# The products of a matmul unit alternate between two PSUM banks instead of filling one bank after the other

## The reference

```python
ada = (c @ w_ada + b_ada)[:, None, :]
sh1, sc1, g1, sh2, sc2, g2 = jnp.split(ada, N_ADA, axis=-1)
u = x * (1 + sc1) + sh1
proj = u @ w_in                                  # 2048 x 8192
z_p, x_c, b_c, c_c, gate_p, gate_c = jnp.split(proj, [o1, o2, o3, o4, o5], axis=-1)
y_p, new_pool = _pool_mixer(z_p, pool_hist, pos, pool_grp_w, pool_scale)
y_p = y_p @ w_pool_up                            # 1024 x 2048
y_c, new_conv = _short_conv(c_c * x_c, conv_hist, conv_w)
y_c = (b_c * y_c) @ w_conv_up                    # 1024 x 2048
mixed = (jax.nn.sigmoid(gate_p) * y_p + jax.nn.sigmoid(gate_c) * y_c) @ w_o
x = _layernorm(ALPHA * x + g1 * mixed, ln1_g, ln1_b)
u2 = x * (1 + sc2) + sh2
h = jnp.square(jax.nn.relu(u2 @ w_ff1 + b_ff1))  # 2048 x 8192
x = _layernorm(ALPHA * x + g2 * (h @ w_ff2 + b_ff2), ln2_g, ln2_b)
```

## Time and profile before

| | |
|---|---|
| median of three runs | 1459.07 us |
| the profiled execution | 1459.57 us, of which its span is 1457.7 |
| mean granted clock of TensorE | 0.997 |
| PE busy | 1442.0 us (99%), 11815 matmuls |
| PEld busy | 1362.0 us (93%) |
| DVE busy | 853.1 us (59%) |
| ACT busy | 531.0 us (36%) |
| POOL busy | 100.6 us (7%) |

### The profile page before, as it was taken

How to read it: one execution, slowest core, us unless ns; L and a number is a source line. 1 busy time by engine, 2 the same in 40 slices (tenths; PEclk the granted TensorE clock), 3 DMA queues, 4 the chain that set the end, 5 groups by cost and what they waited for, 6 DMA issues and landing times.

```text
span 1457.7 us, 27550 instructions
## 1 busy us (share of the span) xinstructions
PE 1442.0 (99%) x11815; PEld 1362.0 (93%) x11815; DVE 853.1 (59%) x1037; ACT 531.0 (36%) x385; POOL 100.6 (7%) x99
## 2 busy tenths in 40 slices
PE   8999999999999999999999999999999999999998
PEld 6899989888888898997899999999999999999997
DVE  4677665565678656449755545454545544454557
ACT  3333223233325223235634333443334433343435
POOL 1000000000440000000050000000000000000800
PEclk9999999999999999999999999999999999999999
DMA  9987888887886786886755555555566555655541
GB/s 316 385 287 275 301 316 311 304 319 274 326 323 245 276 330 245 338 305 233 258 174 179 188 180 173 180 188 180 173 180 187 180 173 181 188 178 173 183 163 61
DMA packets 149727, 343.61 MB, mean 236 GB/s; under 512 B 6037, under 2 KB 16313, under 8 KB 141434
## 3 DMA queue, kind: packets, MB, share of 16 engines
q1 hardware_dynamic: 147986, 340.36, 67.8%
q0 software_dynamic: 752, 1.31, 0.3%
q10 hardware_dynamic: 912, 0.85, 0.2%
HBM read 340.19 MB, written 2.79 MB: 235 GB/s over the span
## 4 chain that ended last, share of the span: by engine, by line
PE 96%; DVE 2%; SPq 1%; DMA 0%; ACT 0%; issue 0%; DVEq 0%; ACTq 0%
PE main L1601 30%; PE main L1602 30%; PE main L1603 30%; PE ps_ada L1635 2%; PE ps_ada L1717 1%; PE ps_adat L1717 1%; PE ps_a L1717 1%; SPq L431 1%; DMA Uf<-in_x_prompt 0%; DVE w_lo L1017 0%; DVE G L1460 0%; ACT w_hi L700 0%; DVE U L1492 0%; DVE G L1454 0%; PE ps_a L1796 0%
## 5 line engine op out<-in xcount | busy, mean ns | idle before, releaser
L1017 DVE TENSOR_TENSOR w_lo<-raw,w_hi 128x2048 fp32r<-128x2048 f32 (+1 forms) x212 | 483.4, 2280 | 458.3 <-ACT w_hi L700 457.8
L700 ACT ACTIVATE w_hi<-raw 128x2048 fp32r<-128x2048 f32 (+1 forms) x227 | 429.8, 1894 | 870.4 <-PE main L1603 856.9
L1601 PE MATMUL main<-U,w_hi 128*128 128x264 f32 x2320 | 662.7, 286 | 3.0 <-issue 1.3
L1603 PE MATMUL main<-U,w_lo 128*128 128x264 f32 x2320 | 660.0, 284 | 0.0
L1602 PE MATMUL main<-U,w_hi 128*128 128x264 f32 x2192 | 621.3, 283 | 0.0
L1601 PEld LDWEIGHTS main<-U,w_hi 128*128 128x128 f32 x2320 | 436.9, 188 | 31.1 <-issue 27.3
L1603 PEld LDWEIGHTS main<-U,w_lo 128*128 128x128 f32 x2320 | 436.4, 188 | 0.0
L1602 PEld LDWEIGHTS main<-U,w_hi 128*128 128x128 f32 x2192 | 413.0, 188 | 0.0
L1601 PE MATMUL main<-H,w_hi 128*128 128x264 f32 x1280 | 365.1, 285 | 0.0
L1603 PE MATMUL main<-H,w_lo 128*128 128x264 f32 x1280 | 362.5, 283 | 0.0
L1602 PE MATMUL main<-H,w_hi 128*128 128x264 f32 x1152 | 327.5, 284 | 0.0
(11 more groups left out here) (271 smaller groups left out, 629.2 us busy)
## 6 DMA issues: line engine op xcount, KB each, us to landing
raw<-in_w_ff SPq DMA_DIRECT2D x128, 1024.0 KB, 5.2
ada_raw<-in_w_ada SPq DMA_DIRECT2D x64, 1024.0 KB, 6.7
raw<-in_w_in SPq DMA_DIRECT2D x63, 1024.0 KB, 9.4
Uf<-in_w_ada SPq DMA_DIRECT2D x18, 1024.0 KB, 9.6
raw<-in_w_o SPq DMA_DIRECT2D x16, 1024.0 KB, 8.9
raw<-in_w_pool_up SPq DMA_DIRECT2D x8, 1024.0 KB, 9.6
raw<-in_w_conv_up SPq DMA_DIRECT2D x8, 1024.0 KB, 9.8
PB<-in_w_ada SPq DMA_DIRECT2D x6, 1024.0 KB, 11.2
```

Of the source, the lines that this page charges most:

```text
L700: nc.scalar.activation(w_hi[:, s % HL, 0:size], raw[:, s, 0:size], ACT.Copy).then_inc(hi_ready, 1)
L1017: tt(w_lo[:, s % HL, 0:size], raw[:, s, 0:size], w_hi[:, s % HL, 0:size].bitcast(F32), ALU.subtract).then_inc(unit_split, 1)
L1601: mm(out, wh, x_hi, start=start, stop=False)
L1603: return mm(out, wl, x_hi, start=False, stop=stop)
```

## The change

`unit` sends every unit that has neither `pieces` nor `early` to a new helper. That helper takes the tiles in pairs, m = 0 and 1, then 2 and 3. Within a pair it goes through the four chunks, and in each chunk issues the six products of both tiles in turn: the high weights of one tile and of the other with x_hi, both again with x_lo, then both low weights with x_hi. So each product goes to the other bank than the one before it. Before a pair that starts a new sum TensorE waits once, for the pair's second bank. `part_done` is counted twice at the pair's end, by the last product of each tile.

```diff
+            def two_tiles(j, t0, m, hi, lo, first, last):
+
+                if first:
+                    pe.wait_ge(psum_free, bank_free(t0 + m + 1))
+                out = [bank[m + e][:, 0:TOK] for e in range(2)]
+                for c in range(KC):
+                    (h0, l0), (h1, l1) = w_of(j % HL, c, m), w_of(j % HL, c, m + 1)
+                    x_hi, x_lo = tile_of(hi[0], hi[1] + c), tile_of(lo[0], lo[1] + c)
+                    start, stop = first and c == 0, last and c == KC - 1
+                    mm(out[0], h0, x_hi, start=start, stop=False)
+                    mm(out[1], h1, x_hi, start=start, stop=False)
+                    mm(out[0], h0, x_lo, start=False, stop=False)
+                    mm(out[1], h1, x_lo, start=False, stop=False)
+                    r0 = mm(out[0], l0, x_hi, start=False, stop=stop)
+                    r1 = mm(out[1], l1, x_hi, start=False, stop=stop)
+                r0.then_inc(part_done, 1)
+                r1.then_inc(part_done, 1)
+
             def unit(j, n, t0, hi, lo, first=True, last=True, early=None, pieces=None):
 
 
 
                 if not pieces:
                     pe.wait_ge(unit_split, split_done(n))
+                if not (pieces or early):
+                    for m in range(0, MT, 2):
+                        two_tiles(j, t0, m, hi, lo, first, last)
+                    return
                 for m in range(MT):
```

## The result

| | before | changed |
|---|---|---|
| median | 1459.07 us | 1465.62 us |
| ratio, 95% interval | | 1.0046 (1.0035 to 1.0056) |
| span of the profiled execution | 1457.7 us | 1464.4 us |
| mean granted clock | 0.997 | 0.998 |

The change makes the kernel 6.6 us slower. The forecast was 1460.9 us with a range from 1455.5 to 1467.0; the time is that of its rival A, 1465.4.

The account below looks back on a forecast made before the run. TensorE was taken to bound the kernel, busy 1442.0 of 1457.7 us. Product cost 0 plus 1.8 us of hand-over waits on the profiled 1459.57 gave 1461.4, or 1460.9 us on the median; range 1455.5 to 1467.0.

Parts of the forecast that it names:

- rival A: Paired units: products dearer because consecutive ones share no stationary tile; 4.5 us on top of 1.8, 1465.4; chance 0.22.
- more than 0.3 ns a product in the ff2 quarters: Sign in the changed profile: a product differing by more than this from 121.3 ns would prove the forecast wrong.
- The alternation is worth nothing: Paired units: sending successive products to another bank changes a product's cost by nothing.
- Rival B: Paired units: adding into a bank not just written is faster; 102 us gain, 1357, a tenth gives 1450.7; chance 0.12.
- the 79 us gain estimated from the Trainium skill: Over 9,024 products: 8.8 ns less each if all excess over 112.5 ns came from staying in one bank; not believed.
- Cost of the new order of reads: Paired units: reading operands in the new order costs 0, ends at -4.5 and +4.5 us.
- Hand-over at ff1 blocks: Turns into ff1 blocks: later evictions make TensorE wait for bank 3; 0.8, 0.1 and, behind ff2, 0.45 us.
- End of the up projections: Where TensorE waits for w_lo: tile 3's multiplication, and TensorE's start with it, come 0.22 us later.
- ff2 block 1 of the last quarter: VectorE is late there: tile 3's later eviction delays w_lo, and TensorE waits 0.27 us.
- So late that it finds all four tiles done and loses nothing: Places outside the listed waits where VectorE runs late: the later hand-over costs nothing.
- TensorE waits for a bank nowhere, so nothing goes: Units waiting for two pairs instead of four banks: no PSUM wait exists to be saved, gain nothing.
- rival D: Pauses at bank changes drop TensorE's clock to 1.2 GHz; for a tenth of the products 90 us, 1551; chance 0.02.

Follow-up runs that it names:

- banks_only: Kernel before with its order of reads kept; only the bank written alternates, both tiles handed over at the pair's end; sums wrong; 1461.54 us, ratio 1.0017.
- woven: Changed kernel's pairs and alternating banks (but for one step), new weight tile each product, moving tiles in the order of the kernel before; 1461.53 us, ratio 1.0017.
- reads_only: Changed kernel's order of reads, but one bank filled after the other, waits and hand-overs tile by tile as before; sums wrong; 1463.93 us, ratio 1.0033.
- threes: Changed kernel's pairs of tiles, but in each chunk three products of one tile, then three of the other; 1462.49 us, ratio 1.0021.

## Why the prediction was right, and where it was wrong

The time lies in the range, but not where the forecast put it: the forecast was to hold from 1458.5 to 1463.5, and 1465.62 falls to rival A, which the range was drawn to take in. The prediction also named what would prove it wrong, more than 0.3 ns a product in the ff2 quarters; it measured 0.36. By its steps:

- *The alternation is worth nothing.* Right, and shown: banks_only and woven have the unit times of the kernel before. The reasons given, `first_chunks` against a plain unit and products of 512 columns, pointed the right way. Rival B is out. So is the 79 us gain estimated from the Trainium skill (TensorE: Matmul & The Clock Gate, section "Wait — 56ns, not 53.3ns?", columns at 2.4 GHz plus about 2.5 ns): no run here came near its 112.5 ns, with or without alternation; a product took 120.6 to 122.8 ns (plain units of 5.787 to 5.893 us).
- *Cost of the new order of reads: 0, with ends at -4.5 and +4.5 us.* This is the term that was mis-sized, and with it the forecast. It measured +4.7 us (reads_only), 0.5 ns a product, a little beyond the upper end. I had seen that a unit's cost depends on its operands' places and took zero because the halves of a quarter have the same mean. But two means of old orders say nothing of a new one. Rival A had the size (1465.4 against 1465.62), but by luck, since its reason was wrong: it blamed the changing stationary tile, and woven changes it at each product for nothing. Nor is it the moving tile read twice; it is the order in which start offsets of the moving tiles follow each other.
- *Hand-over at ff1 blocks.* Forecast 0.13 us for the six turns in quarters 1 and 2, measured by the length of the `first_chunks` unit 0.10 to 0.12; 0.15 behind ff2, measured 0.17; 0.01 to 0.02 in quarters 0 and 3, measured 0 to 0.02. With VectorE's rows above, and with reads_only and threes, where the late hand-over is taken away or shortened and the waits go, these are right by mechanism and size, 1.3 us in all.
- *End of the up projections.* Forecast 0.22, measured 0.22.
- *ff2 block 1 of the last quarter.* Forecast 0.27, measured nothing. Tile 3's eviction came 0.55 us after the unit's start, 0.35 later than before, as forecast. But w_lo came no later, and the reason is that the forecast had the wrong path there. It followed VectorE's own chain, and behind the last eviction stands L1364, which lasts 0.19 us elsewhere. In the kernel before it took 0.71 us here and in the changed one 0.36, and both times it ended 0.05 us after GpSimd's L677. Before:

```profile
1371.81 1.29 POOL L677 TENSOR_TENSOR row_r<-ada_raw,row_hi 35x512 fp32r<-35x512 f32 x1
1372.43 0.71 DVE L1364 TENSOR_TENSOR X<-X,small 128x32 f32<-128x32 f32 x1
```

and in the changed kernel:

```profile
1378.30 1.28 POOL L677 TENSOR_TENSOR row_r<-ada_raw,row_hi 35x512 fp32r<-35x512 f32 x1
1378.62 0.47 DVE L1360 SCALAR_TENSOR_TENSOR X<-main,ada,X 128x256 f32<-128x256 f32 x1
...
1379.27 0.36 DVE L1364 TENSOR_TENSOR X<-X,small 128x32 f32<-128x32 f32 x1
```

In all fourteen traces it ends 0.05 us after that instruction, whether it starts early or late; and of its 18 records in the trace of before this is the only one that overlaps work of GpSimd and the only long one. So GpSimd's instruction set the time of w_lo, and the later evictions only used up a pause. That L1364 is held until L677 ends is read from these rows; no run moved L677 to test it.

- *"So late that it finds all four tiles done and loses nothing."* Wrong. It looked at VectorE alone. Where VectorE is late, TensorE used to start on the first bank freed and now waits for the second too: 0.34 us at the first full unit and 0.52 in the input projection. For the same reason "TensorE waits for a bank nowhere, so nothing goes" was right as far as it goes and missed that a wait can come.
- The sum of waits, 1.8 us, measured 2.3: 0.27 that didn't come, 0.86 that weren't seen, and a little under the forecast elsewhere.
- *Clock.* It stayed (rival D), 1.00 in both halves.

## What to carry to other kernels

When an inner order of matmuls is changed, count two things apart: the hand-over of the sums, which can be worked out from the evictions' rows, and the order in which moving tiles are read, which can't, and must be measured or kept. A pair of sums that ends together gives its reader two tiles at once and asks it for two banks at once; both waits appear where that engine has no slack. And before trying to reorder, try another offset of the buffers: one line, a gap of 128 bytes, took 2.6 us off this kernel (0.9980), where the reorder added 6.6. It is trial only: a gap of 64 bytes cost 9.0 us, and with the reorder the 128 bytes cost 3.5.

## What the runs showed of the hardware that was not expected

- The distance between products of 264 columns at the full clock, about 121 ns, depends on where the moving tiles start in their partition and on the order in which such starts follow each other, over more than the last tile. It repeats to about a nanosecond: single distances in one unit run from 116 to 129 ns and were found again, place by place, in woven. Units of 48 products took from 5.787 to 5.893 us, by nothing but order and a shift of 64 or 128 bytes.
- It does not depend on the PSUM bank, on a bank changing at each product, or on the order of the weight tiles (512 bytes apart): woven and before have the same unit times, 5.813 in ff1 and 5.80/5.85 in ff2.
- A weight tile used twice running is loaded twice (11815 loads for 11815 matmuls) and saves nothing: before has it at every third step, woven never, and the unit times are the same.
- A VectorE instruction on two SBUF tiles that takes 0.19 us by itself (L1364) took 0.36 to 0.77 where it overlapped a GpSimd instruction (L677), and ended 0.05 us after it in all fourteen traces.
